# Ada loads on GpSimd's own queue, and an FFN's last silu of tile 0 in front of the third piece's rounding

## The reference, cut to what matters

```
mod = (silu(c) @ ada_w[l] + ada_b[l]).reshape(B, 3, 3, 1, D)
h   = rmsnorm(x) * (1 + mod[:, j, 1]) + mod[:, j, 0]      # ahead of part j
x   = x + 0.5 * (1 + mod[:, j, 2]) * ((silu(h @ wi_gate) * (h @ wi_up)) @ wo)   # an FFN
```

## Time and profile before

| | us |
|---|---|
| median of 3 runs | 2270.82 |
| the profiled execution | 2266.75 |
| its span, first to last instruction | 2265.0 |
| PE busy | 2151.6 |
| DVE busy | 1637.8 |
| ACT busy | 1071.6 |

### The profile page before, as it was taken

How to read it: one execution, slowest core, us unless ns; L and a number is a source line. 1 busy time by engine, 2 the same in 40 slices (tenths; PEclk the granted TensorE clock), 3 DMA queues, 4 the chain that set the end, 5 groups by cost and what they waited for, 6 DMA issues and landing times.

```text
span 2265.0 us, 28325 instructions
## 1 busy us (share of the span) xinstructions
PE 2151.6 (95%) x10400; PEld 1766.2 (78%) x10400; DVE 1637.8 (72%) x2282; ACT 1071.6 (47%) x1267; POOL 0.2 (0%) x4
## 2 busy tenths in 40 slices
PE   2999989999999995999999999999999999999998
PEld 2877987788788784778888887778888888777887
DVE  6877768777788785688678866577867886757545
ACT  3444533434444455543444447654354444765334
POOL 0000000000000000000000000000000000000000
PEclk9999999999999997999999999999999999999999
DMA  7889523689598642399668854359956895444553
GB/s 311 321 332 341 194 94 134 236 333 336 199 347 317 252 156 86 116 351 336 228 238 331 329 191 139 130 187 344 339 216 249 328 330 185 137 131 148 197 193 130
DMA packets 128256, 537.57 MB, mean 237 GB/s; under 512 B 15024, under 2 KB 15760, under 8 KB 109200
## 3 DMA queue, kind: packets, MB, share of 16 engines
q1 hardware_dynamic: 128144, 536.06, 64.9%
HBM read 534.90 MB, written 1.10 MB: 237 GB/s over the span
## 4 chain that ended last, share of the span: by engine, by line
PE 79%; DVE 10%; DMA 5%; ACT 4%; issue 2%; SPq 1%; ACTq 0%; DVEq 0%
PE GU L1734 13%; PE GU L1738 13%; PE GU L1736 13%; PE PY L1734 10%; PE PY L1738 10%; PE PY L1736 10%; DVE wL L987 2%; ACT wH L560 2%; DMA raw<-in_up_w 2%; DVE ada L1006 2%; PE TM L1783 1%; DMA gates<-gT 1%; PE PY L2066 1%; DMA M<-in_ada_t 1%; DVE x L1066 1%
## 5 line engine op out<-in xcount | busy, mean ns | idle before, releaser
L987 DVE TENSOR_TENSOR wL<-raw,wH 128x2048 fp32r<-128x2048 f32 (+1 forms) x322 | 726.8, 2277 | 260.0 <-ACT wH L560 259.0
L560 ACT ACTIVATE wH<-raw 128x2048 fp32r<-128x2048 f32 (+1 forms) x322 | 604.4, 1900 | 218.7 <-DMA raw<-in_up_w 80.6
L1734 PE MATMUL GU<-wH,xH 128*128 128x512 f32 (+1 forms) x1408 | 556.0, 395 | 13.3 <-DVE xL L1116 11.9
L1738 PE MATMUL GU<-wH,xL 128*128 128x512 f32 (+1 forms) x1408 | 547.1, 389 | 0.0
L1736 PE MATMUL GU<-wL,xH 128*128 128x512 f32 (+1 forms) x1408 | 546.0, 388 | 0.0
L1006 DVE CUSTOM_DVE_ANT_0 ada<-ada,cond 128x1024 f32<-128x1024 f32 x272 | 316.6, 1220 | 0.0
L1734 PEld LDWEIGHTS GU<-wH,xH 128*128 128x128 f32 x1408 | 265.0, 188 | 66.2 <-issue 12.4
L1738 PEld LDWEIGHTS GU<-wH,xL 128*128 128x128 f32 x1408 | 264.7, 188 | 55.6
L1736 PEld LDWEIGHTS GU<-wL,xH 128*128 128x128 f32 x1408 | 265.3, 188 | 51.4
L658 ACT ACTIVATE hH<-TM 128x512 fp32r<-128x512 f32 x80 | 47.9, 599 | 466.1 <-PE TM L1783 465.9
L1734 PE MATMUL PY<-wH,hH 128*128 128x512 f32 x640 | 199.1, 392 | 5.0 <-DVE wL L987 5.0
(11 more groups left out here) (299 smaller groups left out, 2248.7 us busy)
## 6 DMA issues: line engine op xcount, KB each, us to landing
raw<-in_up_w SPq DMA_DIRECT2D x352, 512.0 KB, 6.5
ada<-in_ada_t SPq DMA_DIRECT2D x136, 1024.0 KB, 8.2
raw<-in_down_w SPq DMA_DIRECT2D x176, 512.0 KB, 6.4
raw<-in_c_w SPq DMA_DIRECT2D x96, 512.0 KB, 4.6
raw<-in_a_w SPq DMA_DIRECT2D x40, 512.0 KB, 4.8
raw<-in_b_w SPq DMA_DIRECT2D x32, 512.0 KB, 4.7
M<-in_ada_t SPq DMA_DIRECT2D x8, 1024.0 KB, 12.3
gB<-gates SPq DMA_DIRECT2D x12, 512.0 KB, 5.5
```

Of the source, the lines that this page charges most:

```text
L560: act.activation(wH[:, to, 0:words], raw[:, slot, 0:words], ACT.Copy).then_inc(s_high, 1)
L987: dve.tensor_tensor(wL[:, to, 0:words], raw[:, slot, 0:words], wH[:, to, 0:words], ALU.subtract).then_inc(s_split, 1)
L1734: pe.matmul(outs[i], aH, wh[i], start=first, stop=False)
L1738: ins = pe.matmul(outs[i], aL, wh[i], start=False, stop=last)
```

## The change

It starts when 7 of the 8 start chunks are used, and ahead of the loads of (2,2) it waits, as SP did, until the mixer (2,1) is done. It is not tied to the stage that SP has come to: as soon as DVE has freed a slot the next load is issued, even where it belongs to a later stage. Second, on ACT, in an FFN's last turn, `silu_tile(0)` stands ahead of `cut_third(3)`. The programs of PE and DVE are the same as before.

```diff
                 for n, (k0, lo, width) in enumerate(pieces):
-                    if l == 0 and n in (3, 6):
-                        load_ada(MIXER_CHUNKS[n // 6], 0)
-                        load_ada(MIXER_CHUNKS[n // 6], 1)
                     if n == 10:
                         gate_in(l, 1)
...
-                def loop(first, count, with_ada, c=c0):
+                def loop(first, count):
                     with sp.Fori(0, count) as i:
...
                         load_up(l, j, first + i, 0)
-                        if with_ada and (l, j) == (2, 2):
-                            sp.wait_ge(s_x, NT * (3 * l + 2))
-                        if with_ada:
-                            load_ada(c + i, 0)
                         load_up(l, j, first + i, 1)
-                        if with_ada:
-                            load_ada(c + i, 1)
                         load_down(l, j, first + i - 1)
...
+        @block.gpsimd
+        def _(pool):
+            t = Tally()
+
+            def load_ada(c, q):
+                v = T["ada_t"].rearrange("(c q) p n -> q p c n", q=2)
+                slot = t.next("ada") % ADA_RING
+                pool.wait_ge(s_adafree, t.next(s_adafree))
+                pool.dma_start(ada[:, slot, :], v[q, :, bass.ds(c, 1), :].rearrange("p c n -> p (c n)")
+                               ).then_inc(s_ada[slot], 16)
+
+            pool.wait_ge(s_startfree, 2 * ADA_FIRST - 1)
+            for l, j in PHASES:
+                if (l, j) == (0, 1):
+                    for c in MIXER_CHUNKS:
+                        load_ada(c, 0)
+                        load_ada(c, 1)
+                elif j != 1:
+                    c0, turns = ada_turns(l, j)
+                    if (l, j) == (2, 2):
+                        pool.wait_ge(s_x, NT * (3 * l + 2))
+                    if turns:
+                        with pool.Fori(0, turns) as i:
+                            t.enter(i, [(s_adafree, 2), ("ada", 2)])
+                            load_ada(c0 + i, 0)
+                            load_ada(c0 + i, 1)
+                        t.leave(turns)
...
                 hidden_high()
+                silu_tile(0)
                 if after(l, j):
                     cut_third(3)
-                silu_tile(0)
                 high_tile(0)
```

More of the change, by code:

```diff
@@ L455, in load_cond @@
                 sp.dma_start(cond[:, :], T["cond"][k:k + 1, :].broadcast_to([P, D])).then_inc(s_cond, 16)
[L457 to L462, removed]
             def late_constants():
@@ L481, in ffn @@
                     load_cond(1)
-                c0, turns = ada_turns(l, j)
-                def loop(first, count, with_ada, c=c0):
+                def loop(first, count):
                     with sp.Fori(0, count) as i:
-                        t.enter(i, [(s_split, 3), ("piece", 3), (s_adafree, 2 * with_ada), ("ada", 2 * with_ada)])
+                        t.enter(i, [(s_split, 3), ("piece", 3)])
                         load_up(l, j, first + i, 0)
-                        if with_ada and (l, j) == (2, 2):
-                            sp.wait_ge(s_x, NT * (3 * l + 2))
-                        if with_ada:
-                            load_ada(c + i, 0)
                         load_up(l, j, first + i, 1)
-                        if with_ada:
-                            load_ada(c + i, 1)
                         load_down(l, j, first + i - 1)
@@ L499, in ffn @@
                 for q, c in enumerate(EARLY):
-                    loop(done + 1, c - 1 - done, turns > 0, c0 + done)
+                    loop(done + 1, c - 1 - done)
                     load_up(l, j, c, 0)
-                    if turns:
-                        load_ada(c0 + c - 1, 0)
                     load_up(l, j, c, 1)
-                    if turns:
-                        load_ada(c0 + c - 1, 1)
                     if after(l, j):
@@ L512, in ffn @@
                         late_constants()
[L513 to L517, removed]
+                loop(done + 1, NF - 1 - done)
                 gate_out(l, j)
```

## The result

The changed kernel takes 2274.36 us, the median of 20 runs (2265.4 to 2282.31); the kernel before, beside it on the same chip, 2268.59 us (20 runs, 2264.39 to 2274.26). The ratio is 1.003, with a 95% interval of 1.0019 to 1.004. That is 6 us slower by the two medians and 7 by the ratio, where I had forecast 2 us faster. A second set of runs gave 1.0036 (1.002 to 1.0051). The profiled execution took 2274.51 us, 7.8 more than that of before, and the loss of clock is part of it: the mean granted clock is 0.986 where it was 0.99. Over all 20 runs of the change it is 0.9868 on average, and 0.9881 to 0.9885 in the four later sets of before.

What follows compares the result with a forecast made beforehand. PE was taken as the bound, with the DMA engines close behind inside the FFNs. Terms of 1.1 + 1.4 - 0.3 made 2.2 us saved, taken as 2, giving 2269 us; the 8-in-10 range was 2262 to 2291.

Steps and rivals of the forecast that it cites:

- Edit 2, 3.3 us: Silu moved ahead of the third piece's rounding: 1.1 us saved at each end of (0,0), (1,0), (3,0).
- Edit 1, 0 in the 66 turns: Moving ada loads from SP to GpSimd was priced at 0 in the 66 FFN turns with ada loads.
- (a): Ada load in an FFN turn: it may be about 6 us later than now before PE feels it.
- (b): Down piece in an FFN turn: 4.2 us of slack, and 0.6 us more before PE.
- The cover: In FFN turns with ada loads, PE's own work, 16.8 us a turn without idling, hides changes in load timing.
- Edit 1, the third piece later by 1.4 us at three ends: Ends of (0,0), (0,2), (1,0): a GpSimd ada load delays the third piece by 1.4 us, between 0 and 2.8.
- evenly: If ada load and third piece share the DMA engines evenly, about half of 2.8 us falls before the piece.
- The sooner gate write: Ends of (0,0) and (1,0): with ada loads off SP's queue, gates reach DRAM some 1 us sooner.
- the 1.1 us in hand: End of (0,2): low_tile ends at 584.2 and PE comes to down_last at 585.30, leaving 1.1 us spare.
- 1: Rival, FFN turns with ada loads: DMA engines become the bound, 0.4 us more a turn, 26 us in all; 12%.
- 2: Rival: a piece or ada load is late in the turn; 0.3 us a turn makes 20 us, 2289; 12%.
- 4: Rival: third piece later by 2.8 us eats edit 2's gain, 4 us slower, 2275; 10%, plus 3% for more.

Runs made afterwards that it cites:

- the second edit alone: The kernel before, all loads still on SP, with only silu_tile(0) moved ahead of cut_third(3): 2263.93 us, ratio 0.9981.

## Why the prediction was wrong, step by step

- *What bounds the kernel.* Right: PE does, and SP's 424.1 us cost nothing. With the harm of the early loads taken away, GpSimd's queue gives nothing over the second edit alone.
- *Edit 2, 3.3 us.* Right: 4 us, interval 2 to 7. Its working was too careful. By its own figures waits of 1.1, 0.4 and 0.8 us for `hL` would be left (2.21, 1.47 and 1.90 less 1.1 each; my list of signs says "about 1.1" at all three, which doesn't follow). They were 0.14, 0 and 0.46 us at the three ends of the second edit alone. I had held the third piece's landing fixed against PE's turn; it lands earlier or later by about 1 us from run to run.
- *Edit 1, 0 in the 66 turns.* **This is the step that failed.** The slacks (a) and (b) are those of an ada load and of a down piece, read from one turn of (0,2). That of an up piece I never read, and the trace of before shows that it is the smallest. In that very turn ACT idles until the up piece has landed, and it does so 42 times in all (the second row: us in total, times, longest):

```profile
448.95 1.92 ACT L560 ACTIVATE wH<-raw 128x2048 fp32r<-128x2048 f32 x1 [0.71 <-DMA raw<-in_up_w]
```

```profile
ACT wH L560 <- DMA raw<-in_up_w: 80.6, 42, 5.0
```

  The cover, "PE idles nowhere in such a turn", came from a stretch in (2,2). The turn behind the late constants is not like it: five small transfers stand ahead of its up piece, which took 11.7 us already, and PE waited 0.70 us for it. There was no slack to hide 2 us, and 3.49 us of idle time came out. Holding these two loads alone gave back 7 to 8 us, holding those at the ends alone 8, and both together all of edit 1's 10. The two single gains add up to more than the whole, so they are not separate costs; why, these runs don't show.
- *Edit 1, the third piece later by 1.4 us at three ends.* The mechanism was right, and the size too small: +0.0 at (0,0), +2.1 at (0,2), +2.2 at (1,0), inside the bound of 2.8. Two loads follow the piece within 3.5 us, not one, which is the likely reason that "evenly" was the wrong middle. The sooner gate write, which I set against it by 1 us at (0,0) and (1,0), came there: from the issue of the write to that of the reading back it is 4.5 us instead of 6.3, and 5.4 instead of 6.4. At (0,2) it went the other way (5.18 us in the chain of waits below, 4.31 in the earlier trace rows). There the piece is issued 1.1 us later against PE's turn and lands 2.1 us later, so its rounding starts 3.2 us later, past the 3 us that I had named as a sign of being wrong. Less the 1.1 us in hand that is 2.1 us, and PE waited 2.17.

```profile
569.37 5.18 DMA gates<-gT
```

- *The sum, term by term.* In the profiled pair PE's waits changed by these amounts, in us saved: 2.2 at (0,0) (forecast 0.7), -0.4 at (1,0) (0.7), 1.9 at (3,0) (1.1), -2.2 at (0,2) (-0.3), and -2.8 behind the constants (0). The four ends make 1.5 where I had 2.2, so that in this pair the missing fifth term turns the sum around.
- *The price of an idle us.* The prediction took it as 1 us and had no term for the clock. Added idle time costs 1.2 to 1.4. In the profiled pair the clock is the larger part: the waits changed by 3.5 + 4.1 - 5.6 - 0.7 = +1.3 us, and five stretches of 1.6 us are 8; the two make 9.3 for the 7.6 us by which the span grew. One pair is partly luck, since the number of stretches varies. Over all runs the clock is 0.0016 lower, by an estimate 0.0016 x 2270 = 3.6 us, about half of the 6 to 7.
- *The rivals.* 1 did not happen: the DMA share in the stretch is 0.91. 2 happened, but in single turns and not in each: the up piece behind the constants is its case, as its own "others have less" says, and a new wait of 0.65 us for `wL` stands at 744.57, in (1,0). 4's mechanism happened too. I had given them 12% and 13%, and priced 4 at 4 us from the worst case of the piece alone. That 2274 us lies inside my range of 2262 to 2291 is no merit of the sum: the far part of the range was there for losses in every turn. The Trainium skill's rule ("DMA: Bandwidth & Descriptors", Issuing engines are not separate DMA queues) says that such loads run on the same 16 engines and interleave, and the late pieces agree. Its other half, that issuing from several engines only saves the sequencer's time, led me to the 0. Another issuer also changes when each load enters, and here the change of issuer cost 10 us.

## What to carry to other kernels

Freeing a queue from a wait moves loads earlier, and a load that comes early takes DMA time from the piece that is needed first. Read the slack of every kind of load, and look for the turns with the least of it (behind odd transfers, at stage ends), not at a typical one. Before an edit that saves issue time, check whether the critical load can simply be issued sooner: here the third piece ahead of the gates took away the waits at all ends, on one queue and on two. And where PE is the bound, price its idle time above one for one, and read its busy time together with the granted clock.

## What I had not expected of the hardware

- A stretch at half clock lasts 3.4 us here, with matmuls 0.43 us apart instead of 0.23. One stood behind waits of 3.49 and 1.88 us, and none behind one of 2.17. Its number in a trace ran from 12 to 17 and did not follow the time: 16 in the second edit alone, 12 in the slower kernel before.
- The moment of a later load decides when an earlier piece lands: behind the constants 13.6 to 15.4 us with the second ada load 3.1 to 3.9 us behind it, 10.0 to 11.7 us with 6.0 or more.
- Loads issued by GpSimd land no later than SP's in this kernel: a median of 7.2 us for 1 MB, where SP's took 8.2.
- Late pieces go with a wide spread of the whole kernel: 17 us over the runs of the change, 5 us with its loads held at all places.
